# Router by chunks, a gather split among the experts, two more weight slots

## What is computed

```python
def expert_choice_ffn(h, w_router, w_gate, w_up, w_down):
    cap = CAPACITY_FACTOR * S // N_EXPERTS            # 32 of 256 tokens, 16 experts
    aff = jax.nn.softmax((h @ w_router).astype(jnp.float32), axis=-1)
    gates, idx = lax.top_k(aff.transpose(0, 2, 1), cap)
    xe = h[bidx, idx]
    hg = jnp.einsum('becd,edf->becf', xe, w_gate)
    hu = jnp.einsum('becd,edf->becf', xe, w_up)
    y = jnp.einsum('becf,efd->becd', jax.nn.silu(hg) * hu, w_down)
    y = y * gates[..., None].astype(y.dtype)
    return jnp.zeros_like(h).at[bidx, idx].add(y)
```

## Time and profile before

| | |
|---|---|
| median of 3 runs | 1964.46 us (1959.02, 1965.06, 1964.46) |
| profiled execution | 1961.58 us, its span 1959.8 us |
| mean granted clock of TensorE | 0.906 of full speed |
| busy: TensorE, weight loads, VectorE, ScalarE, GpSimd | 86%, 62%, 22%, 13%, 1% |
| HBM read | 391.31 MB, 201 GB/s over the span |
| chain that ended last | TensorE 73%, DMA 20%, VectorE 4% |
| of it, `ring<-in_w_experts` | 20% |

### The profile page before, as it was taken

One profiled execution on the slowest core, in us unless ns is written; L12 is line 12 of the kernel. 1 busy time (PEld: TensorE's weight loads), 2 busy tenths in 40 slices (PEclk: granted clock), 3 DMA queues, 4 the chain that ended last, 5 costly groups with the idle time before them and its releaser, 6 DMA issues.

```text
span 1959.8 us, 20358 instructions
## 1 busy us (share of the span) xinstructions
PE 1680.5 (86%) x8952; PEld 1212.6 (62%) x8952; DVE 436.9 (22%) x1035; ACT 254.6 (13%) x599; POOL 22.1 (1%) x43
## 2 busy tenths in 40 slices
PE   6998999999998889999999899998987566665655
PEld 5766688888875566788888788767673112112111
DVE  4512013330012321023300355652122000000001
ACT  1222021000000321110000122221001000000000
POOL 0000000000000000000000001000000000000000
PEclk9989999999999799999999799997798878788787
DMA  9412423664434023326753201342343999999997
GB/s 378 151 44 110 148 86 136 266 239 174 161 112 146 0 87 129 129 86 236 278 191 143 86 1 44 108 123 94 122 179 129 427 427 427 428 428 427 428 428 331
DMA packets 42823, 395.24 MB, mean 202 GB/s; under 512 B 15856, under 2 KB 18288, under 8 KB 19056
## 3 DMA queue, kind: packets, MB, share of 16 engines
q1 hardware_dynamic: 42032, 392.46, 50.9%
q0 software_dynamic: 272, 1.05, 0.2%
q10 hardware_dynamic: 432, 0.44, 0.1%
HBM read 391.31 MB, written 2.62 MB: 201 GB/s over the span
## 4 chain that ended last, share of the span: by engine, by line
PE 73%; DMA 20%; DVE 4%; issue 1%; ACT 1%; ACTq 0%; DVEq 0%
PE pb L418 65%; DMA ring<-in_w_experts 20%; PE pb L493 6%; PE pb L572 1%; DVE rstd L1486 1%; DMA small_w<-in_small_w 1%; ACT arena L1174 1%; DVE arena L1553 0%; DVE hT L1497 0%; DVE hT L1498 0%; DVE arena L1533 0%; DVE arena L1682 0%; DVE arena L1679 0%; DVE arena L1631 0%; DVE arena L1680 0%
## 5 line engine op out<-in xcount | busy, mean ns | idle before, releaser
L418 PE MATMUL pb<-hT,ring 128*128 128x256 f32 x2368 | 526.8, 383 | 8.9 <-DVE hT L1491 8.9
L418 PEld LDWEIGHTS pb<-hT,ring 128*128 128x128 f32 x2368 | 451.5, 192 | 78.9 <-issue 18.1
L418 PE MATMUL pb<-ring,arena 128*32 128x256 f32 (+3 forms) x2208 | 319.5, 638 | 137.6 <-DMA ring<-in_w_experts 132.4
L418 PE MATMUL pb<-arena,ring 128*128 128x256 f32 (+3 forms) x1600 | 315.0, 365 | 16.0 <-DVE arena L1631 9.8
L418 PEld LDWEIGHTS pb<-arena,ring 128*128 128x128 f32 (+2 forms) x1600 | 274.4, 190 | 55.0 <-DVE arena L1631 10.6
L418 PEld LDWEIGHTS pb<-ring,arena 128*32 128x32 f32 (+2 forms) x2208 | 102.8, 139 | 326.3 <-DMA ring<-in_w_experts 185.4
L1174 ACT ACTIVATE arena<-pb 128x512 f32<-128x512 f32 (+3 forms) x194 | 93.9, 487 | 893.0 <-PE pb L418 764.8
L418 PE MATMUL pb<-arena 64*128 64x128 f32 (+3 forms) x448 | 114.7, 398 | 18.1 <-ACT arena L1174 8.6
L493 PE MATMUL pb<-arena,ring 128*128 128x256 f32 x512 | 127.4, 401 | 1.0 <-ACT arena L1174 1.0
L493 PEld LDWEIGHTS pb<-arena,ring 128*128 128x128 f32 x512 | 98.9, 199 | 22.4 <-issue 7.6
L418 PEld LDWEIGHTS pb<-arena 64*128 64x128 f32 (+2 forms) x448 | 69.2, 187 | 58.1 <-issue 40.9
(11 more groups left out here) (216 smaller groups left out, 849.4 us busy)
## 6 DMA issues: line engine op xcount, KB each, us to landing
ring<-in_w_experts SPq DMA_DIRECT2D x96, 2048.0 KB, 26.4
ring<-in_w_dense SPq DMA_DIRECT2D x86, 2048.0 KB, 8.4
ring<-in_w_dense SPq DMA_DIRECT2D x2, 1536.0 KB, 6.6
cons<-in_cons SPq DMA_DIRECT2D x1, 1808.0 KB, 19.8
xT<-in_xT SPq DMA_DIRECT2D x1, 1024.0 KB, 6.2
side<-in_memT POOLq DMA_DIRECT2D x1, 1024.0 KB, 6.4
out<-xT SPq DMA_DIRECT2D x4, 256.0 KB, 2.2
lru_w<-in_lru_w SPq DMA_DIRECT2D x1, 512.0 KB, 16.1
```

Of the source, the lines that this page charges most:

```text
L418: return nc.tensor.matmul(o, l, r, start=st, stop=sp)
```

## The change

- Slots: the ring's six are joined by two in the arena (numbers 4096 to 8191 and 0 to 4095), and the experts go through eight slots in turn. The first load into the arena waits for `dn_ready` 2; the last of the eight takes over the wait for the last dense unit.
- Router: per chunk both token tiles, so all is done when the last chunk is.
- `shifted_norm`: VectorE scales (`hs_ready`), ScalarE adds the shift (`shift`), for `n1` and `n2`; no link.
- Gather: in four groups of four experts, each group in two halves of four chunks, so that one instruction is 128 columns wide instead of 512. Group 0 stands before the loop; the other six halves follow the `gate_up` of experts 0 to 5, in bank 2, and ScalarE evacuates them between `tanh` and `ht`. `h2t` and `xe` move to other buffers, as do the experts' small tiles.
- Tables: after the roots of `xa0`, `cd`, `xa1`, after the root of the LRU and after the shift of `n2`, ScalarE makes an exponential of one column that nobody reads (`warm`).
- Top-k: one copy of the affinities instead of two.

```diff
+        h2t, xe = (lru_w_, rtp), (view(hTt, 0, 4, 512), view(arena, 8192, 4, 512))
+        rw = [more[0:NE, S * i:S * (i + 1)] for i in range(4)]
...
+        def slot_at(i):
+            return (ring, i * UNIT) if i < SLOTS else ((arena, 4096), (arena, 0))[i - SLOTS]
...
-        ESLOT = [ASLOT, TSLOT, R1, LSLOT, R0, GSLOT]
+        ESLOT = [ASLOT, TSLOT, SLOTS, R1, SLOTS + 1, LSLOT, R0, GSLOT]
...
-                slot_of.append(ESLOT[j])
+                slot_of.append(ESLOT[(NU * e + j) % len(ESLOT)])
...
-            for t in range(TT):
-                for k in range(DC):
-                    if t == 0:
-                        ready(k)
-                    last = mm(ps[:, 16 * t:16 * t + 16], hT[:, k, t * P:(t + 1) * P], w_rt[:, k, :], k == 0, k == DC - 1)
+            for k in range(DC):
+                ready(k)
+                for t in range(TT):
+                    last = nc.tensor.matmul(ps[:, 16 * t:16 * t + 16], hT[:, k, t * P:(t + 1) * P], w_rt[:, k, :],
+                                            start=k == 0 and t == 0, stop=k == DC - 1, skip_group_check=True)
...
-            for c in range(DC):
-                ps = fill(f"xe{c}")
-                for t in range(TT):
-                    last = mm(ps, h2t[:, t, c * P:(c + 1) * P], Ph[:, t, :], t == 0, t == 1)
-                mark(last, f"xe{c}")
-            copied(pe, *(f"xe{c}" for c in range(DC)))
+            def gather(g, i, b=None):
+                ps = fill(f"xe{g}{i}", b)
+                for c in range(4):
+                    for t in range(TT):
+                        last = mm(ps[:, c * P:(c + 1) * P], h2t[t][:, (4 * i + c) * P:(4 * i + c + 1) * P],
+                                  Ph[:, t, g * P:(g + 1) * P], t == 0, t == 1)
+                mark(last, f"xe{g}{i}")
+            gather(0, 0)
+            gather(0, 1)
...
             for e in range(NE):
                 turn_gates(e)
+                if e % EG == 0:
+                    copied(pe, f"xe{e // EG}0", f"xe{e // EG}1")
                 gate_up(e)
+                if e < 6:
+                    gather(1 + e // 2, e % 2, 2)
                 turn_hidden(e)
...
-                before = NDENSE - 1 if u == NDENSE + NU - 1 else last_in(slot_of[u], u)
+                before = NDENSE - 1 if u == NDENSE + len(ESLOT) - 1 else last_in(slot_of[u], u)
...
+                if u == NDENSE + 2:
+                    sp.wait_ge(dn_ready, 2)
...
+                if tag in ("xa0", "cd", "xa1"):
+                    fn(warm, eps, ACT.Exp)
...
+            def shift(at):
+                for c in range(DC):
+                    shifted[0] += 1
+                    act.wait_ge(hs_ready, shifted[0])
+                    fn(hT[:, c, :], hT[:, c, :], ACT.Identity, bias=modc[:, at + c:at + c + 1]).then_inc(h_ready, 1)
...
             root("n2")
+            shift(24)
+            fn(warm, eps, ACT.Exp)
...
-                    link(V.scalar_tensor_tensor(hT[:, c, :], xT[:, c, :], gain[:, c:c + 1], rs[:, :], ALU.mult, ALU.mult))
-                    V.tensor_scalar(hT[:, c, :], hT[:, c, :], modc[:, shift + c:shift + c + 1], None, ALU.add).then_inc(h_ready, 1)
+                    V.scalar_tensor_tensor(hT[:, c, :], xT[:, c, :], gain[:, c:c + 1], rs[:, :], ALU.mult, ALU.mult
+                                           ).then_inc(hs_ready, 1)
...
-            V.tensor_copy(rw[0], ps[0:NE, 0:S])
-            V.tensor_copy(rw[1], ps[0:NE, 0:S]).then_inc(free, 1)
+            V.tensor_copy(rw[0], ps[0:NE, 0:S]).then_inc(free, 1)
```

More of the change, by code:

```diff
@@ L240, in program @@
         dnT = view(arena, 3072, 4, S)
-        h2t, xe = view(arena, 0, 2, 1024), view(arena, 2048, DC, 512)
-        rw = [arena[0:NE, 6144 + S * i:6144 + S * (i + 1)] for i in range(4)]
+        h2t, xe = (lru_w_, rtp), (view(hTt, 0, 4, 512), view(arena, 8192, 4, 512))
+        rw = [more[0:NE, S * i:S * (i + 1)] for i in range(4)]
         Ph, Pq = view(arena, 10240, 2, 512), view(side, 1024, 2, 2 * P)
-        tg, hg = view(arena, 7168, 2, S), view(arena, 7680, 2, S)
-        hgT, yq, PGq = view(arena, 8192, 2, 2, P), view(arena, 8704, 2, S), view(arena, 9216, 2, S)
+        tg, hg = view(side, 0, 2, S), view(side, 512, 2, S)
+        hgT, yq, PGq = view(side, 1536, 2, 2, P), view(arena, 11264, 2, S), view(arena, 11776, 2, S)
         sat = [0]
@@ L266, in program @@
         aff, selc, raff = small(2, NE), small(2, NE), small(2)
-        top8 = small(8)
+        top8, warm = small(8), small(1)
         units = [(a["w_dense"][u], *size) for u, size in enumerate(plan[0])]
@@ L298, in program @@
                 units.append((a["w_experts"][NU * e + j], D, 512))
-                slot_of.append(ESLOT[j])
+                slot_of.append(ESLOT[(NU * e + j) % len(ESLOT)])
         nth = [slot_of[:u + 1].count(slot_of[u]) for u in range(len(units))]
         sga, sgd = view(ring, GSLOT * UNIT, DC, S), view(ring, GSLOT * UNIT + DC * S, DC, S)
-        loaded = [sem(f"slot_loaded{i}") for i in range(SLOTS)]
+        loaded = [sem(f"slot_loaded{i}") for i in range(SLOTS + 2)]
         filled = [sem(f"bank_filled{i}") for i in range(8)]
@@ L618, in gate_up @@
                         for q in range(4):
-                            last = mm(ps[quad(q), :], xe[:, 2 * m + k, e * CAP:(e + 1) * CAP], w[:, k, q, :],
+                            last = mm(ps[quad(q), :], xe[m // 2][:, 2 * (m % 2) + k, e * CAP:(e + 1) * CAP], w[:, k, q, :],
                                       m == 0 and k == 0, m == 3 and k == 1)
@@ L1121, in _ @@
                 n = nr // P * ncol
-                sp.dma_start(ring[:, at:at + n], w[:, 0:n]).then_inc(loaded[slot_of[u]], 16)
+                sp.dma_start(t[:, at:at + n], w[:, 0:n]).then_inc(loaded[slot_of[u]], 16)
                 if u == GATES_AT + 1:
@@ L1343, in _ @@
             root("n1")
+            shift(0)
             def head_squares(dst, src_):
@@ L1460, in _ @@
                 for i in range(2):
-                    copy(f"h2_{t}{i}", h2t[:, t, 512 * i:512 * (i + 1)])
-            for c in range(0, DC, 2):
-                copy(f"xe{c}", xe[:, c, :])
+                    copy(f"h2_{t}{i}", h2t[t][:, 512 * i:512 * (i + 1)])
+            copy("xe00", xe[0][:, :, 0:P], fours)
             for e in range(NE):
@@ L1467, in _ @@
                 fn(tg[:, e % 2, :], ps[:, 0:S], ACT.Tanh, scale=0.5).then_inc(eth_ready, 1)
+                if e < 6:
+                    g, i = 1 + e // 2, e % 2
+                    copy(f"xe{g}{i}", xe[i][:, :, g * P:(g + 1) * P], fours)
                 copy(f"ht{e}", hgT[:, e % 2, :, :], lambda ps: ps[:, 0:S].rearrange("p (c n) -> p c n", c=2))
@@ L1918, in _ @@
             ps, free = full(dve, "affT")
-            V.tensor_copy(rw[0], ps[0:NE, 0:S])
-            V.tensor_copy(rw[1], ps[0:NE, 0:S]).then_inc(free, 1)
+            V.tensor_copy(rw[0], ps[0:NE, 0:S]).then_inc(free, 1)
             copied(dve, "affT")
             for r in range(CAP // 8):
-                link(V.max(top8[0:NE, :], rw[1]))
-                link(V.match_replace(rw[1], top8[0:NE, :], rw[1], -1.0))
+                now = rw[0] if r == 0 else rw[1]
+                link(V.max(top8[0:NE, :], now))
+                link(V.match_replace(rw[1], top8[0:NE, :], now, -1.0))
             link(V.tensor_tensor(rw[3], rw[1], rw[0], ALU.not_equal))
@@ L1949, in _ @@
             gated(1)
-            for c in range(1, DC, 2):
-                ps, free = full(dve, f"xe{c}")
-                V.tensor_copy(xe[:, c, :], ps).then_inc(free, 1)
+            ps, free = full(dve, "xe01")
+            V.tensor_copy(xe[1][:, :, 0:P], fours(ps)).then_inc(free, 1)
             for e in range(NE):
```

16 lines of the change are left out of this document (9 added, 7 removed).

## The result

| | before | after |
|---|---|---|
| median | 1963.62 us (1959.02 to 1965.06, 4 runs) | 1928.51 us (1927.24 to 1930.25, 4 runs) |
| ratio | | 0.9826, 95% interval 0.9807 to 0.9844 |
| profiled execution, span | 1961.58, 1959.8 | 1927.24, 1925.4 |
| mean granted clock | 0.906 | 0.922 |

The change took 35.1 us off the median, and 34.3 from one profiled execution to the other. The forecast was 26.9, and the measured time lies 1.5 us under the range.

The account below looks back on a forecast made before the run. Expert units were taken as transfer-bound at 4.9 us each after the first expert's first read, with compute bounding before it. Terms summed to 26.9: 1961.58 - 26.9 = 1934.7, plus 2.9 for the median gives 1937.5 us, range 1930 to 1945.

Parts of the forecast that it names:

- the slots: Expert weight stream: two more units loaded before the first expert leave 88 instead of 90, gaining 9.8 us.
- in the steady state nothing else comes of it: Expert stream after its restart: extra slots gain nothing more, since the transfer never waited for a slot there.
- n1: First norm: with the shift on ScalarE the last chunk begins near 1115.4 instead of 1117.37, gaining 1.9 us (1.5 to 2.1).
- from there the chain is TensorE's own: Behind the norm's last chunk only TensorE sets the time, so the gain stays 1.9 us.
- the tables: Early Exp loads: 0.45 us at the softmax of `dil`, 0 at `xa0`, `xa1`, `fox`; bound for these three 0 to 1.3.
- Rival C: Expert stream: eight queued transfers make each unit dearer, 1973 us at 0.4 us a unit; chance 0.03.
- Rival B: Expert slots: the two extra loads come too late and are still under way at the restart, 1947 us; chance 0.06.
- Gather: Ahead of the first expert: 32 narrow instructions take 6.0 us, first `gate_up` after 6.85 instead of 18.02, gaining 11.2.
- Rival A: Gather: weight loads are not hidden under narrow matmuls, 14.4 us instead of 6.0, total 1946; chance 0.07.
- Router: Second norm's chunks: both token tiles per chunk end near 1466.9 to 1467.2 against 1470.44, gaining 3.2 us (2.1 to 5.3).
- the clock falls at about 1463, so four chunks at 0.5: Router matmuls: four chunks at full clock at 0.5 us and four at 0.9, behind the 3.2 us gain.
- rival D: Router and gather: denser work holds TensorE at 2.4 GHz, total about 1932 us; chance 0.10.

## Why the prediction failed

The path was right: the first read of the first expert, the number of units left then, and compute ahead of it. Three terms were sized too small. For the slots it was the step "in the steady state nothing else comes of it" (9.8 forecast, 11.0 measured). For n1 it was "from there the chain is TensorE's own", which left out that an earlier norm moves the falls of TensorE's clock behind it (1.9 forecast, 3.7 measured). For the tables it was the same omission behind `dil` (0.45 forecast, 1.8 measured). The rest of the miss is in no term: most of it is how this set of executions fell.

**Slots: right mechanism, sized at 9.8, measured 11.0.** From the first expert to the end it is 447.6 to 449.4 us in the seven profiles with eight slots and 458.7 to 460.4 in the six with six. The 9.5 to 11.2 behind the landing of the last unit differ with the clock; up to that landing it is 438.1 to 438.6 against 449.2 to 449.4. The two units are 9.8 of it. The step that failed was "in the steady state nothing else comes of it": 88 units cost 0.016 us less each, 1.4 us, with eight queued. I had looked only for gaps, and there were none. Rival C, that depth makes a unit dearer, has the opposite sign of what happened. Rival B is out: 88 units stand behind the restart in the DMA records.

**Gather: 11.2 forecast, 11.6 in the first pair.** The 32 narrow instructions ended 5.4 us after the start, 6.0 in the sum, since the full clock was back after 3.3 us and not 4.3. In the other profiles of the changed kernel and its variants with this gather the first expert follows its start after 6.4 to 7.2 us, by the clock, around the 6.85 of the sum. From the last sums of n2 to the restart the profiles of the changed kernel took 28.7 to 29.9, the one with the router's edits alone 41.28: 11.3 to 12.5 for gather and copy, where 11.5 was forecast, and the spread is the clock under router and gather. Rival A, unhidden weight loads, is out: at the full clock a pair starts every 0.22 us (1476.28 to 1476.50 above), so an instruction costs 0.11. By these rows narrow against wide is 0.26 (0.11 against 0.43).
The Trainium skill, "TensorE: Matmul & The Clock Gate", section "Back-to-back issue gap", gives 81 ns for 128 columns against 131 ns for 512, which makes a ratio of 0.62 as an estimate. These fp32 rows don't bear it out.

**Router: 3.2 forecast, 2.3 measured in the profile of the result** (root to the router's end 12.72 before, 10.44 after). The failed step is "the clock falls at about 1463, so four chunks at 0.5". It fell 1.4 us before the first chunk in the profile after, and all 32 instructions ran at 0.22. That is close to my lower bound of 2.1. The size hangs on that fall: the same stretch is 10.44 to 10.45 in four profiles with these edits and 8.8 to 9.3 in the other six, a gain of 3.4 to 3.9, where the row of 32 is 5.3 to 5.9 long instead of 6.98. So the forecast lies between the two, and rival D, a kinder clock at router and gather, came in part in six executions, but not in the profile of the result.

**One copy: 0.34 forecast, 0.33 measured** from VectorE's first copy to the one-hot (7.22 before, 6.89 after). The transposes ahead of it and the turn took 0.5 longer at half clock, so from the router's end to the gather's start it doesn't show in this pair (12.0 and 12.2); the run with the router's edits alone, at the same half clock but with two copies, took 12.5. **Early table at the router: 0, right.** The transposes were late, exactly as told.

**n1: 1.9 forecast, 3.7 measured.** By the eighth matmul of `dk` it is 2.9, in every profile with the shift (9.90 to 9.93 against 12.80 to 12.81). 2.4 are the 32 instructions, which go on at 0.22 us without a gap for a chunk. I had up to 0.50 a chunk and a later first one. The other 0.5 is the clock, which is back sooner behind them: the stretch at 1.2 GHz that starts near 1110 lasts 10.2 us in all ten profiles with the shift and 13.7 in the four without. Then the fall near 1242 stays out, 1.6 more, of which 0.8 is lost again to later falls. The step that failed is "from there the chain is TensorE's own".

**Tables: 0.45 forecast at `dil`, 0.46 measured there, 1.8 with the clock behind it.** The matmuls from 628 to 735 us (places of the kernel before) took 105.4 to 106.2 us in the nine profiles with the tables, 105.9 on the mean, and 106.9 to 108.0 in the five without, 107.7 on the mean. The time at 1.2 GHz in that stretch was 34.1 us in all nine and 37.5 in all five, though it is cut into other pieces from one execution to another. Tables alone on the kernel before and tables removed from the changed one agree in this, so the tables buy it. The load of 1.28 us in the row of the router's own run is followed by its exponential 0.01 us later there as well, and where the engine had been busy before a load, the load came 0.02 us after the last instruction.
The Trainium skill, "ScalarE: Activation LUTs", section "What ACT_TABLE_LOAD costs", adds a drain of about 1.38 us to a load. These rows don't show it on either side of the load.

**Not in the sum: the execution itself.** When the last runs were planned, I had 29.9 us of terms that repeat: 2.9 (n1), 14.4 (second norm to restart, 13.7 to 15.0 by profile), 11.0 (slots) and 1.6 (tables). With 3.7 for n1 and 1.8 for the tables they make 30.9. Over all executions taken, twelve of the changed kernel have a mean of 1932.0 and 49 of the kernel before 1963.8: 31.9. The three comparisons gave 35.1, 27.4 and 30.7. I added 2.9 "to the median" and allowed 3 us for how executions differ. The start alone is 5.2 us wide, and from the first matmul to the last sums of n2 the changed kernel and those with its dense part took 1427.0 to 1435.4 us, once 1418.9. The first four runs of the changed kernel all lay at 1927 to 1930, and the eight later ones at 1931 to 1936. The time was missed by 9.0 us: 4.0 are sizes (30.9 against 26.9), 1.0 stays open (31.9 against 30.9), 3.2 are that set of runs (35.1 against 31.9), which is luck, and 0.8 the median I started from (1964.46 against 1963.62).

**Open:** whether the change moves other falls of the clock too. The long one near 1350 lasts 37.5 us in all five profiles of the kernel before and its variants; in the nine of the changed kernel and its variants it lasts 34.1 in five, 37.5 in three, and is missing once. Where it lasts 34.1, the way from n1 to the sums of the second norm is another 2.9 to 3.2 us shorter (347.1 to 347.4 against 350.3). The 33.4 with the start mended on both sides speak for more than 30.9, the 30.7 of the same call against it. The falls near 104, 552 and 863 come and go in both kernels.

## What to carry to other kernels

When a transfer-bound stage follows a compute-bound one, ask how many units are loaded when it starts and when the first slot comes free; here each unit more was worth 5.5 us, 4.9 of it its own transfer, and a microsecond off router or gather was worth one. Split work by who needs it first: with the gather of the first four experts alone the first expert began after 6.4 us instead of 18.2, and the rest hid under the transfer. And before an edit of 0.3 to 2 us is costed, take several profiles of the unchanged kernel: the terms that repeat to 0.1 us can be summed, the rest is the range. Then follow the same matmul, counted from the start, through all profiles: a fall of the clock that is missing in each profile with an edit and there in each without belongs to the edit, as the one near 1242 did, and one that comes and goes in both belongs to the range. The cheapest gain of the study was none of the planned ones: one wait that holds the 2 MB loads back until three small ones have landed, 10 to 12 us.

## What the runs showed of the hardware

- A small load of one queue, issued beside the first 2 MB loads of another, landed with the large one that was issued just before or beside it: 10.6 to 10.7 us after issue in the four profiles that issued it at 1.69 us, 15.3 to 16.3 in the seven that issued it at 1.85. With the large ones held back it took 5.5 to 6.0.
- Units of 2 MB cost 4.914 us with six slots in turn, 4.903 with seven and 4.898 with eight.
- TensorE's fall to 1.2 GHz in the same code came or stayed out, or changed its length, between executions of one kernel: none or 6.8 us near 552, 6.8 or 13.7 near 104 (3.4 or 6.8 with the start mended). Once there was almost none where the thirteen other profiles have 34.1 or 37.5 us, with TensorE 95% busy in that window (97% in the profile of the result, nearly 100% in the kernel before).
- Other falls follow the code: 3.4 us near 1242 in four of four profiles without the shift of n1, and in none of the ten with it.
- A fp32 instruction of 128 columns, with a weight load of its own, cost 0.11 us at 2.4 GHz and 0.21 at 1.2 GHz, where one of 512 columns cost 0.43 at 2.4 GHz.
